# Weight parts laid 32 bytes further in their slots for the units of 256 columns

## What is computed

```
h = rmsnorm(x, norm1_g[l]);  pre = h @ w_in[l]                 # 13336 columns
x = x + (gated sum of y_hg @ w_br_hg, y_ml @ w_br_ml, y_mb @ w_br_mb) @ w_out
x = x + (silu(gate) * val) @ w_down,   gate, val = conv(rmsnorm(x) @ w_up)
for i in range(2):                                             # second block
    z = modulate(rms_norm(x), ...) @ w_in_2[i]                 # and of the 256 context tokens
    x = x + g1 * (concat(out_a, out_b, out_c) @ w_out_2[i])
    x = x + g2 * conv_ffn(modulate(rms_norm(x), ...), w_up_2[i], w_down_2[i])
```

## Time and profile before

| | |
|---|---|
| median of three runs | 1666.59 us |
| span of the profiled execution | 1665.4 us |
| instructions | 34323 |
| TensorE matmuls | 14687, of them 9792 from `product` |
| TensorE busy | 1609.8 us, 97% |
| LDWEIGHTS busy | 1441.5 us, 87% |
| VectorE, ScalarE, GpSimd busy | 73%, 53%, 12% |
| mean granted TensorE clock | 0.992 |

### The profile page before, as it was taken

One profiled execution on the slowest core, in us unless ns is written; L12 is line 12 of the kernel. 1 busy time (PEld: TensorE's weight loads), 2 busy tenths in 40 slices (PEclk: granted clock), 3 DMA queues, 4 the chain that ended last, 5 costly groups with the idle time before them and its releaser, 6 DMA issues.

```text
span 1665.4 us, 34323 instructions
## 1 busy us (share of the span) xinstructions
PE 1609.8 (97%) x14687; PEld 1441.5 (87%) x14687; DVE 1213.9 (73%) x2054; ACT 876.9 (53%) x1335; POOL 199.4 (12%) x124
## 2 busy tenths in 40 slices
PE   8999999999999999999988999999999998899999
PEld 7999888898999999997766888888877786699999
DVE  4374499577777886577766788877888769568864
ACT  5435645548546666445675544323433456666653
POOL 4303540000000110100000111110110100041100
PEclk9999999999999999999999999999999999999999
DMA  7655555454455555521102233464344323045544
GB/s 278 243 218 225 202 207 185 166 219 170 147 185 192 194 181 173 188 97 65 52 2 97 86 149 141 161 217 152 127 167 175 133 77 102 2 161 198 199 164 140
DMA packets 41128, 259.65 MB, mean 156 GB/s; under 512 B 4368, under 2 KB 7696, under 8 KB 14480
## 3 DMA queue, kind: packets, MB, share of 16 engines
q1 hardware_dynamic: 40976, 257.46, 43.1%
HBM read 256.39 MB, written 1.05 MB: 155 GB/s over the span
## 4 chain that ended last, share of the span: by engine, by line
PE 70%; DVE 20%; ACT 4%; DMA 3%; issue 2%; POOL 1%; DVEq 0%; SPq 0%; ACTq 0%
PE acc_psum L208 20%; PE acc_psum L210 19%; PE acc_psum L209 19%; DVE w_low_sb L173 4%; DVE mod_products L335 3%; DVE u_filtered L2074 2%; DVE ring_sb L335 2%; PE acc_psum L217 2%; PE acc_psum L2521 2%; PE acc_psum L2547 1%; DMA ring_sb<-in_w_up 1%; DMA ring_sb<-in_w_in 1%; ACT w_high_sb L161 1%; PE acc_psum L271 1%; POOL w_low_sb L173 1%
## 5 line engine op out<-in xcount | busy, mean ns | idle before, releaser
L208 PE MATMUL acc_psum<-h_high_sb,w_high_sb 128*128 128x256 f32 (+1 forms) x2176 | 655.7, 301 | 7.9 <-DVE h_low_sb L497 2.6
L209 PE MATMUL acc_psum<-h_low_sb,w_high_sb 128*128 128x256 f32 (+1 forms) x2176 | 647.6, 298 | 0.0
L210 PE MATMUL acc_psum<-h_high_sb,w_low_sb 128*128 128x256 f32 (+1 forms) x2176 | 647.5, 298 | 0.0
L161 ACT ACTIVATE w_high_sb<-ring_sb 128x1024 fp32r<-128x1024 f32 (+2 forms) x412 | 387.0, 989 | 366.7 <-PE acc_psum L210 218.2
L173 DVE TENSOR_TENSOR w_low_sb<-ring_sb,w_high_sb 128x1024 fp32r<-128x1024 f32 (+1 forms) x358 | 390.9, 1134 | 109.2 <-ACT w_high_sb L161 99.7
L208 PEld LDWEIGHTS acc_psum<-h_high_sb,w_high_sb 128*128 128x128 f32 x2176 | 411.2, 189 | 35.8 <-issue 13.3
L209 PEld LDWEIGHTS acc_psum<-h_low_sb,w_high_sb 128*128 128x128 f32 x2176 | 410.5, 189 | 15.5 <-issue 0.5
L210 PEld LDWEIGHTS acc_psum<-h_high_sb,w_low_sb 128*128 128x128 f32 x2176 | 410.3, 189 | 14.9
L173 POOL TENSOR_TENSOR w_low_sb<-ring_sb,w_high_sb 128x1024 fp32r<-128x1024 f32 x54 | 132.0, 2470 | 672.9 <-ACT w_high_sb L161 672.9
L2074 DVE SCALAR_TENSOR_TENSOR u_filtered<-acc_psum,par_sb,u_filtered 128x255 f32<-128x255 f32 (+2 forms) x264 | 150.7, 571 | 43.2 <-ACT u_filtered L2211 23.7
L208 PE MATMUL acc_psum<-u_high,w_high_sb 128*128 128x256 f32 (+1 forms) x528 | 168.3, 319 | 4.9 <-DVE w_low_sb L173 3.2
(11 more groups left out here) (312 smaller groups left out, 1870.4 us busy)
## 6 DMA issues: line engine op xcount, KB each, us to landing
ring_sb<-in_w_in SPq DMA_DIRECT2D x68, 1024.0 KB, 6.6
ring_sb<-in_w_up SPq DMA_DIRECT2D x66, 1024.0 KB, 4.9
ring_sb<-in_w_down SPq DMA_DIRECT2D x48, 704.0 KB, 4.2
ring_sb<-in_w_ada SPq DMA_DIRECT2D x24, 1024.0 KB, 4.8
ring_sb<-in_w_ada_rows SPq DMA_DIRECT2D x24, 1024.0 KB, 4.8
ring_sb<-in_w_out SPq DMA_DIRECT2D x12, 1024.0 KB, 4.8
ring_sb<-in_w_br_hg SPq DMA_DIRECT2D x4, 1024.0 KB, 6.8
ring_sb<-in_w_br_ml SPq DMA_DIRECT2D x4, 1024.0 KB, 4.9
```

What stands on the lines that cost most here:

```text
L161: self.nc.scalar.activation(self.high[:, self.shifted(c, g, piece)], self.ring[:, c % RING, piece], ACT.Copy)\
L208: nc.tensor.matmul(out, sh, mh, start=start, stop=False)
L209: nc.tensor.matmul(out, sh, ml, start=False, stop=False)
L210: return nc.tensor.matmul(out, sl, mh, start=False, stop=stop)
```

## The change

Four constants. The parts of TOKENS_STAND and NARROW units begin 8 floats (32 bytes) further in their slot: 32 and 160 bytes in, where it was 0 and 128. Those of WIDE units stay 64 bytes in. The slots stand 2080 floats (8320 bytes) apart, 128 bytes less. The two tensors keep their size (2 * 2048 + 96 floats), so that no other tensor moves. Modulo 128 bytes the two slots of a tensor have the same place before and after; modulo 256 bytes they had the same before and are 128 apart after. No instruction, wait or transfer is added, removed or reordered.

```diff
-SLACK = 64
-TOKENS_STAND, WIDE, NARROW = 0, 16, 32
+SLACK = 32
+TOKENS_STAND, WIDE, NARROW = 8, 16, 40
+PARTS = 2 * SLOT + 96
...
-        self.high = self.sbuf("w_high", [P, 2 * SLOT + SLACK + NARROW], F32R)
+        self.high = self.sbuf("w_high", [P, PARTS], F32R)
...
-        self.low = self.sbuf("w_low", [P, 2 * SLOT + SLACK + NARROW], F32R)
+        self.low = self.sbuf("w_low", [P, PARTS], F32R)
```

## The result

The changed kernel took 1684.85 us (median of four runs, 1682.94 to 1688.22), the kernel before 1665.34 us beside it (1660.41 to 1667.74). The ratio is 1.012, with a 95% interval from 1.0095 to 1.0146: slower by 1.2%. The span of the profiled execution is 1683.2 us, against 1665.4. In the changed kernel the line of `PARTS` moves the code down by one, so that L208, L209, L210, L161 and L173 of before are L209, L210, L211, L162 and L174.

The account below looks back on a forecast made before the run. The prediction took TensorE's distance between matmul starts as the bound. Gains of 4.9 us (feed-forwards) and 5.4 us (mixer, input projections) make 10.3, so 1666.6 becomes 1656.3, forecast as 1656.5 us; range 1653 to 1693 us.

Parts of the forecast that it names:

- What bounds the kernel: Whole kernel: TensorE, busy 97% of the span, sets the time, through the distance between matmul starts rather than listed durations.
- That the place of the two tiles to each other picks the pace: Matmuls of 256 columns: distance from moving to standing tile modulo 128 gives 113.4 or 117.7 ns at 64, 120.0 at 0.
- locked to each other: Matmuls at distance 64: the pace is a state between loads and moving stream, chosen anew at each pause.
- What it costs today: Slow 256-column matmuls cost 12.1 us: 4.9 in the feed-forwards, 2.5 in the mixer, 4.7 in the input projections.
- three quarters: Share of the gain counted in mixer and input projections, where products alternate with waits on VectorE and ScalarE: 5.4 us.
- The pace at 96 and 32: NARROW at 96, TOKENS_STAND at 32: all 256-column units at 113.4 ns or nearly so, gaining 10.3 us; chance 0.42.
- the clearest sign of a gain: Down projection of the last layer: its 176 listed matmuls would go from 49.4 to 48.6 us.
- Rival one: All 256-column units, feed-forwards above all: slower, as 64 is farthest from bad 0; 1678 to 1700 us; 0.40 with rival two's reverse.
- all at 117.7: Rival one's case with every 256-column matmul at 117.7 ns: 21.4 us more than today, 18 on the path, 1685 us.
- The fourth part: Slots 128 bytes closer: second slot differs modulo 256; 840 matmuls of 512 columns could lose 5.5 us, kept for the range.
- Its last sign: Matmuls of 512 columns should keep 226.5 ns.
- The other engines: Split's write (L161) and subtraction (L173) keep 1050 and 1220 ns; shift costs nothing, up to 2.5 us for the range.

Follow-up runs that it names:

- the maps: Two runs giving single unit pairs their own places, one with slots 8320 bytes apart, a finer one in 4-byte steps on the kernel before: 1676.32 and 1676.51 us.
- the 32 bytes alone: Kernel before with all weight parts 32 bytes later except WIDE's, which stay; slots still 8448 bytes apart: 1682.95 us, ratio 1.0103.
- the copy: The kernel before without any edit, timed against itself: 1662.52 us, ratio 0.9986.
- the control: Kernel before with the 32-byte `first_gain` moved behind `w_low_sb`, so `par_sb`, `con_sb` and `X_sb` move but no product operand does: 1663.12 us, ratio 0.997.
- the slots alone: Kernel before with slots 8320 bytes apart in place of 8448, places within the slot unchanged: 1663.73 us, ratio 0.9984.
- NARROW at 76: Kernel before with every NARROW unit at distance 76 bytes modulo 256 from the activations, in both slots: 1655.46 us, ratio 0.9948.

## Why the prediction was wrong

The forecast was 1656.5 us, 10 us faster than before; measured were 1684.85 us, 19.5 us slower.

**What bounds the kernel: right.** The distance between starts is what the time follows. TensorE's excess rose from 13.1 to 39.3 us, and the last product matmul starts 17.7 us later in the span.

**That the place of the two tiles to each other picks the pace: right.** It was one lead out of the built program's addresses and is shown by the two experiments that moved the activations, with the weights and without them. That the loads and the moving stream are then "locked to each other" is a picture that no run shows.

**What it costs today: right.** The prediction read 12.1 us of matmuls off the best pace out of the durations of one line; measured on all starts, the stages of 256 columns hold 11.8. It gave the 507 matmuls of 455 to 635 us to the feed-forward, though 155 of them belong to the mixer; at three quarters instead of the whole this is less than 0.4 us of its sum.

**The pace at 96 and 32: here it failed.** The step is the forecast's "the shift takes the two streams out of each other's way, all units of 256 columns run at 113.4 ns or nearly so": a price for two places of which the prediction itself says that "no row of the trace shows" them. In the kernel after, NARROW units run at 117.9 ns at 96 (slot 0) and 116.8 at 224 (slot 1), TOKENS_STAND ones at 118.4 at 32 and 119.8 at 160, and none of them ever at 113.4. In place of a gain of 12.1 us of matmuls, 10.3 of them on the path, the units of 256 columns lost 21.3. Of the two bounds, 113.4 and 120.0, the price at 96 lay at two thirds and that at 32 at three quarters. The forecast took 64 for the edge of a bad region; the maps show no regions at all, but a few single good distances (64, 76, 88, 192) with bad ones 4 bytes away. Two stretches at 64 and one at 0 said that 64 is good part of the time, and that should have weighed more than a picture of edges: to leave a place that is known to be partly good for one that isn't known is a draw from all places, and most of those turned out bad.

The place named as the clearest sign of a gain, the last down projection, did get faster (49.4 to 49.2 us in the listed line, 62.95 to 62.59 from first to last start). It is no sign of 113.4 ns: it stood at the slow pace of 64, 117.8 ns, and now runs at 117.5 and 116.7 in its two slots.

**Rival one: right in size, partly by luck.** Its case "all at 117.7" gave 1685 us, 18 more than 1666.6; measured were 1684.85, 19.5 more than the 1665.34 beside it. The pace is an average of parts that differ: NARROW 117.3 on average over its slots, TOKENS_STAND 119.1 over its own; weighted by 6066 and 1611 matmuls that is 117.7. Its reason, 64 as the farthest point from a bad 0, was not right: 76 is better than 64, and 88 is fast where 72, nearer to 64, took 118.3. Its excess was right too: it had 21.4 us more in the units of 256 columns, and the traces have 26.2 in all less 4.9 in the WIDE stage, 21.3.

**The fourth part: right, and in the wrong place.** "Modulo 256 the second slot now stands otherwise": the prediction named up to 5.5 us for the WIDE units of slot 1, and they lost 5.8 ns each, 4.9 us in all. It left that out of the sum, though, and read every row modulo 128. Distance 0 and distance 128 differ by 5.8 ns at 512 columns, so a period of 128 is wrong. Its last sign, that the 512 column matmuls should keep 226.5 ns, held in slot 0 alone.

**What lies on the path.** Up projections counted whole, as told: excess +3.8 us, stage +3.75. The WIDE stage gave half (excess +4.9, stage +2.6). The mixer seems to give less than three quarters (excess +9.4, stage +4.0), but the two traces differ in something else too. Busy times, then granted clock, DMA share and GB/s, from 300 to 310 us, before and after:

```profile
300.00:310.00 10.00, 10.00 (x53) 8.52 (x52) 2.98 (x5) 1.70 (x4) 0.00 (x0) 0.66 0.56 216
```

```profile
300.00:310.00 10.00, 9.27 (x70) 7.57 (x59) 6.33 (x9) 4.86 (x8) 0.00 (x0) 1.00 0.82 315
```

The kernel before had a stretch here in which the granted clock was 0.66 on average, and after hadn't: TensorE's lower level, 1.2 GHz, for 6.8 of the 10 us, worth 3.4 us. Just ahead of it, from 295.0 to 300.3 us, TensorE had been busy for 3.7 of 5.3 us. Both have such stretches elsewhere. Between 224 and 330 us they add up to 13.7 us before, 10.2 after and 3.4 with the 32 bytes alone (mean clock 0.94, 0.95 and 0.98). Half of that is an estimate of what they cost; taken off each mixer it leaves 492.1, 497.9 and 501.4 us: +5.7 for +9.4 of excess, and +9.2 for +11.0, or 0.61 and 0.84. Equal mixers don't agree better than that: by the same estimate the mixers of the copy, the control and the slots alone stand at 491.7, 493.6 and 495.7 us with 4.7, 5.9 and 6.4 us of excess. So the three quarters of the prediction fit, and the traces don't settle the share further. Outside the WIDE stage 15.2 of 21.3 us came through in the profiled executions, 0.71, where the prediction used 0.85 (18 us). The WIDE stage's 2.6 us, which the rival hadn't counted, made up for it; that is the luck in its 1685.

**The other engines: right.** In the stages of the earlier trace rows L162 takes 1049 to 1059 ns after (L161 1050 to 1058 before) and L174 1220 to 1222 (L173 the same before), so the shift cost them nothing.

**The two pages of the Trainium skill** that were named would have made the sum zero. "TensorE: Matmul & The Clock Gate", section "What happens when you issue a matmul", lets loads of the standing tile take nothing from the moving stream; here the same instructions cost 113.4 to 120.9 ns by where their two operands lie to each other, so the runs don't agree that the two are independent; what they share, no run shows. The 16-byte cachelines in the table at the head of "SBUF — State Buffer" don't explain it either: the starts at distances 72 and 76 lie in the same 16 bytes and take 118.3 and 113.5 ns, those at 84 and 88 do too and take 119.9 and 114.3.

**What stays open.** Why 64, 76, 88 and 192 are good, and which event at a pause chooses the pace. The load of a standing tile runs under the matmul ahead of it, and all tiles of a kind start at the same place modulo 256; so it is open too whether a matmul's own two tiles count or a load and its neighbour's stream. Nor do the runs say how many bits of the address matter beyond 256 bytes: within a stage the tiles lie whole multiples of 512 bytes apart and the pace held.

## What to carry to other kernels

When TensorE is the bound and equal matmuls show more than one distance between starts, look up where the two operands start in a partition and sweep that distance in small steps, many distances in one execution, with the roles kept; don't extrapolate from two points. Judge a place by how often it falls to its worse pace, not by its best one, since the pace is drawn anew in each execution. And compare small gains with an unedited copy: here such a copy read 0.14% under its own original, and a control with the same distances in all products 0.3%.

## What the runs showed of the hardware

- Back to back and at full granted clock, an fp32r matmul of 256 columns with its own load of the standing tile takes between 113.3 and 120.9 ns from start to start, by the distance of its operands' starts modulo 256 bytes, in steps as small as 4 bytes; with 512 columns it is 226.7 to 234 ns. With the weights standing 76 is good nearly always, 64 and 88 part of the time, and most of the 44 distances tried never.
- A shift of all tensors together by 32 bytes shows no effect (ratio 0.9994, 0.9973 to 1.0015), nor does the place for the splits on ScalarE and VectorE (copies of 1024 columns 1049 to 1059 ns, subtractions 1220 to 1222 in the places of before and after).
- Some distances have two paces: 64 has 113.3 and 117.8 ns, 88 has 113.3 and 116.7, and 96 was seen at 117.4 and 118.7. A pace mostly lasts until a pause, and is drawn anew in each execution: 25 runs of the kernel before on one chip spread from 1656.41 to 1672.63 us, 8 runs of NARROW at 76 from 1653.89 to 1658.33.
- The same distance can be good for one role and bad for the other: 76 takes 113.6 ns with the weights standing and 120.9 with the activations standing.
